# A hybrid S5 / SSD / mLSTM layer: other order of the S5 block's small products, one tile less transposed, S5 steps one slot later

## What is computed

```python
p = h @ W_in                                   # u, z, xbc, dt, qk, v, i, f, o
xbc = silu(causal_conv(xbc, conv_w, conv_b))   # 768 channels x, 256 of B, 256 of C
cb     = einsum('bclgn,bcsgn->bclsg', cm, bm)          # C enters channel-major
states = einsum('bcsgn,bcsgj,bcsgjp->bcgjpn', bm, decay_end, xdt)   # B and x token-major
y_off  = einsum('bclgn,bcgjpn,bclgj->bclgjp', cm, h_prev, exp(acs)) # C channel-major
bu_re  = einsum('blgh,gph->lbgp', ug, bb_re)   # S5: inputs to the states, then a scan
y      = einsum('lbgp,ghp->blgh', s_re, c_re) - einsum('lbgp,ghp->blgh', s_im, c_im)
```

## Time and profile before

| | |
|---|---|
| runs | 2896.5, 2898.15, 2898.3 us; median 2898.15 |
| the profiled execution | 2895.86 us, its span 2894.0 us |
| busy, share of the span | PE 98%, PEld 80%, DVE 66%, ACT 41%, POOL 13% |
| mean granted clock of TensorE | 0.994 of full |
| transfers | 545 MB, mean 188 GB/s |

### The profile page before, as it was taken

How to read it: one execution, slowest core, us unless ns; L and a number is a source line. 1 busy time by engine, 2 the same in 40 slices (tenths; PEclk the granted TensorE clock), 3 DMA queues, 4 the chain that set the end, 5 groups by cost and what they waited for, 6 DMA issues and landing times.

```text
span 2894.0 us, 36039 instructions
## 1 busy us (share of the span) xinstructions
PE 2846.0 (98%) x13576; PEld 2304.7 (80%) x13576; DVE 1903.5 (66%) x2616; ACT 1191.6 (41%) x2005; POOL 386.0 (13%) x496
## 2 busy tenths in 40 slices
PE   8999999999999989999999999999999999999998
PEld 5888888777777767888888788888888888888887
DVE  7677887666853358887343776666866655656656
ACT  6222222454443445545333533333533333545543
POOL 0000000012530236664121100000000000000000
PEclk9999999999999999999999999999999999999999
DMA  4222443446665958887878654444542223866862
GB/s 162 73 73 86 135 132 112 145 143 203 222 198 159 299 173 279 278 300 272 303 268 332 239 197 164 168 153 165 172 172 94 106 98 138 333 194 210 285 195 103
DMA packets 294569, 545.14 MB, mean 188 GB/s; under 512 B 59228, under 2 KB 150780, under 8 KB 284924
## 3 DMA queue, kind: packets, MB, share of 16 engines
q1 hardware_dynamic: 262636, 437.69, 45.2%
q0 software_dynamic: 24704, 75.52, 6.9%
q10 hardware_dynamic: 7056, 29.63, 2.6%
HBM read 358.30 MB, written 184.44 MB: 188 GB/s over the span
## 4 chain that ended last, share of the span: by engine, by line
PE 47%; DVE 2%; DMA 1%; ACT 1%; issue 1%; SPq 0%; DVEq 0%; ACTq 0%
PE f_banks L2985 25%; PE f_banks L2993 14%; PE f_banks L2087 7%; DMA f_h_raw<-hq 1%; PE f_banks L2290 0%; DMA f_bop2lo<-hq 0%; DVE f_snap L2788 0%; DVE f_w_op L2762 0%; DVE f_a L2800 0%; ACT f_w_op L2624 0%; DVE f_a L2795 0%; ACT o_late L2191 0%; ACT f_snap L2642 0%; DVE f_raw L2776 0%; DVE f_bop2lo L2755 0%
## 5 line engine op out<-in xcount | busy, mean ns | idle before, releaser
L2993 PE MATMUL f_banks<-f_d_op 128*128 128x512 f32 x1848 | 419.0, 389 | 0.0
L2993 PEld LDWEIGHTS f_banks<-f_d_op 128*128 128x128 f32 x1848 | 347.1, 188 | 71.8
L2832 DVE TENSOR_TENSOR f_d_op<-f_d_raw,f_d_op 128x1024 fp32r<-128x1024 f32 x154 | 187.4, 1225 | 149.0 <-ACT f_d_op L2663 148.4
L674 PE MATMUL t_banks<-h_hi,c_w_hi 128*128 128x512 f32 x640 | 254.5, 398 | 0.0
L1900 PE MATMUL t_banks<-t_w_hi,h_hi 128*128 128x512 f32 (+1 forms) x640 | 247.9, 387 | 5.1 <-DVE t_w_lo L1761 4.3
L674 PE MATMUL t_banks<-h_hi,c_w_lo 128*128 128x512 f32 x640 | 250.0, 391 | 0.0
L674 PE MATMUL t_banks<-h_lo,c_w_hi 128*128 128x512 f32 x640 | 249.3, 389 | 0.0
L2663 ACT ACTIVATE f_d_op<-f_d_raw 128x1024 fp32r<-128x1024 f32 x154 | 162.8, 1061 | 198.3 <-PE f_banks L2993 161.5
L1900 PE MATMUL t_banks<-t_w_lo,h_hi 128*128 128x512 f32 (+1 forms) x640 | 237.7, 371 | 0.0
L1900 PE MATMUL t_banks<-t_w_hi,h_lo 128*128 128x512 f32 (+1 forms) x640 | 236.8, 370 | 0.0
L2642 ACT ACTIVATE f_snap<-f_banks 128x1024 f32<-128x1024 f32 x88 | 90.3, 1026 | 253.6 <-PE f_banks L2985 253.6
(11 more groups left out here) (410 smaller groups left out, 6293.3 us busy)
## 6 DMA issues: line engine op xcount, KB each, us to landing
f_raw<-in_w_gu SPq DMA_DIRECT2D x88, 512.0 KB, 6.3
sop<-f_a SPq DMA_DIRECT2D x154, 256.0 KB, 2.0
f_d_raw<-sop SPq DMA_DIRECT2D x154, 256.0 KB, 2.9
t_raw<-in_w_tok SPq DMA_DIRECT2D x72, 512.0 KB, 4.6
f_d_raw<-top SPq DMA_DIRECT2D x88, 256.0 KB, 4.4
m_bc<-rows SPq DMA_DIRECT2D x16, 1152.0 KB, 6.8
f_d_raw<-in_w_dn SPq DMA_DIRECT2D x66, 256.0 KB, 3.1
o_y_lo<-y_lo SPq DMA_DIRECT2D x16, 1024.0 KB, 7.8
```

Source lines behind the costliest of these rows:

```text
L674: last = nc.tensor.matmul(banks[:, p % RING, :], w[:, n % 2, k, :], h[:, q, k, :], start=k == 0 and j == 0, stop=k == KD - 1 and j == 2)
L2832: tt(d_op[d % D_RING][:, 2:4], d_raw[:, d % S_RING], d_op[d % D_RING][:, 0:2].bitcast(F32), sub).then_inc(dlo_ok, 1)
L2993: last = nc.tensor.matmul(banks[:, bank, :], d_op[d % D_RING][:, s, tok], d_op[d % D_RING][:, w, :], start=k == 0 and j == 0, stop=k == FU ...
```

## The change

It has three parts. First, two loops of small products are nested the other way, so that consecutive matmuls alternate between the lane groups. The first is in the setup of the lag kernels, the second in `states_in`. Second, tile 8 of the conv tiles (`NOT_TOK = 8`, C of SSD group 0) is no longer transposed, copied and stored; the tiles after it move up one place, `tok_dram` has 11 tiles (`CTT = 11`) and the load of it 1408 columns where it had 1536. Third, `S5_SLOT` is 53.

```diff
-UT, CT, CTT = 4, 16, 12
+UT, CT, CTT = 4, 16, 11
+NOT_TOK = 8
+    def token_piece(c):
+        m, q = divmod(c, BLK)
+        return None if m == NOT_TOK or m > CTT else c if m < NOT_TOK else c - BLK
...
         def transposes(c):
-            if c // BLK < CTT:
+            i = token_piece(c)
+            if i is not None:
                 pe.wait_ge(silu_ok, c + 1)
-                if c >= 2:
-                    pe.wait_ge(tok_ok, c - 1)
+                if i >= 2:
+                    pe.wait_ge(tok_ok, i - 1)
                 for a in range(4):
-                    last = nc.tensor.transpose(tr_banks[:, c % 2, a * P:(a + 1) * P],
+                    last = nc.tensor.transpose(tr_banks[:, i % 2, a * P:(a + 1) * P],
...
-                for g in range(2):
-                    lanes = slice(g * S5P, (g + 1) * S5P)
-                    for q in range(2):
-                        for r, b_in in enumerate((bbr, bbi)):
+                for q in range(2):
+                    for r, b_in in enumerate((bbr, bbi)):
+                        for g in range(2):
+                            lanes = slice(g * S5P, (g + 1) * S5P)
                             last = nc.tensor.matmul(k_banks[g][:, q, :],
...
-X_C, B_C, K_C = 0, XW, XW + NG * NS + NS
+X_C, B_C, K_C = 0, XW, XW + NG * NS
...
-            sp.dma_start(tk[c % 2][:], tok_dram[c * P:(c + 1) * P, :]).then_inc(in_[c % 2], 16)
+            sp.dma_start(tk[c % 2][:, 0:CTT * P], tok_dram[c * P:(c + 1) * P, :]).then_inc(in_[c % 2], 16)
...
-    S5_SLOT, S5_STEP = 52, 2
+    S5_SLOT, S5_STEP = 53, 2
...
-                for e in range(2):
-                    lanes = slice(e * S5P, (e + 1) * S5P)
-                    for r in range(2):
+                for r in range(2):
+                    for e in range(2):
+                        lanes = slice(e * S5P, (e + 1) * S5P)
                         last = nc.tensor.matmul(in_bank[lanes, b, r, :], ...
```

More of the change, by code:

```diff
@@ L254, in send_tok @@
         def send_tok(c):
-            m, q = divmod(c, BLK)
-            if m < CTT:
-                sp.wait_ge(tok_ok, c + 1)
+            i = token_piece(c)
+            if i is not None:
+                m, q = divmod(i, BLK)
+                sp.wait_ge(tok_ok, i + 1)
                 sp.dma_start(tok_dram[q * NB:(q + 1) * NB, m * P:(m + 1) * P].rearrange("(a p) m -> p a m", p=P),
-                             tok[:, c % 2].rearrange("p (a m) -> p a m", m=P)).then_inc(tok_sent[c % 2], 16)
+                             tok[:, i % 2].rearrange("p (a m) -> p a m", m=P)).then_inc(tok_sent[i % 2], 16)
         for q in range(BLK):
@@ L434, in taps @@
             if c >= RING:
-                if m - 1 < CTT:
-                    dve.wait_ge(tr_ok, c - RING + 1)
+                before = token_piece(c - RING)
+                if before is not None:
+                    dve.wait_ge(tr_ok, before + 1)
                 if m - 1 >= CH0:
@@ L448, in token_major @@
         def token_major(c):
-            if c // BLK < CTT:
-                dve.wait_ge(tr_ok, c + 1)
-                if c >= 2:
-                    dve.wait_ge(tok_sent[c % 2], 16 * (c // 2))
-                nc.vector.tensor_copy(tok[:, c % 2], tr_banks[:, c % 2, :]).then_inc(tok_ok, 1)
+            i = token_piece(c)
+            if i is not None:
+                dve.wait_ge(tr_ok, i + 1)
+                if i >= 2:
+                    dve.wait_ge(tok_sent[i % 2], 16 * (i // 2))
+                nc.vector.tensor_copy(tok[:, i % 2], tr_banks[:, i % 2, :]).then_inc(tok_ok, 1)
         tt, ts, stt = nc.vector.tensor_tensor, nc.vector.tensor_scalar, nc.vector.scalar_tensor_tensor
@@ L817, in mixer_memory @@
         part = sb("part", [P, 2, NB])
-        tk1, zo1, va1 = sb("tk1", [P, CTT * P]), sb("zo1", [P, XW + VW]), sb("va1", [P, HM, DA])
+        tk1, zo1, va1 = sb("tk1", [P, (CTT + 1) * P]), sb("zo1", [P, XW + VW]), sb("va1", [P, HM, DA])
         inter, num = sb("inter", [P, 2, HP, DA]), sb("num", [P, 2, HP, DA])
```

2 lines of the change are left out of this document (1 added, 1 removed).

## The result

| | before | changed |
|---|---|---|
| runs, median | 2897.32 us (2896.28 to 2898.3, 4 runs) | 2911.73 us (2910.72 to 2915.81, 4 runs) |
| profiled execution, its span | 2895.86, 2894.0 us | 2910.72, 2908.8 us |
| mean granted clock of TensorE | 0.994 | 0.992 |

The account below looks back on a forecast made before the run. The prediction took TensorE, busy 98% of the span, as the bound. Its terms -1.7 - 3.5 - 1.1 + 2.5 + 2.4 + 0.8 made -0.6 us; 2895.9 - 0.6 + 2.3 = 2897.5 us, range 2891.5 to 2904.

Parts of the forecast that it names:

- (c): SP's S5 loads: u late behind two weight halves in seven steps, 0.35 us each, +2.5 us (0 to +7).
- (d): GLU, fixed at slot 90: TensorE waits longer for g, +2.4 us (ends +1.0 and +2.8).
- (e): TensorE's clock falls to half speed after the longer wait for g, +0.8 us (ends 0 and +1.7).
- Transposes: Tile 8's four pieces lose their transposes on TensorE, 0.43 us each: 1.7 us less.
- lag kernels: Lag kernel setup: alternating lane groups pair at once, 0.44 us a set, eight sets: 3.5 us less (0 to 4.2).
- `states_in` alternating: Inputs to the states: the pairs are there already, so 0, at most 0.2 us either way over 16 steps.
- (a): First S5 step: one slot later, u has long landed and TensorE's wait goes, 1.1 us less.
- (b): VectorE splits both weight halves before every other S5 step, yet states start on time: 0, end +0.5 us.
- The S5 loads become the bound of every other step: Rival for the S5 steps: each of seven u loads 1.0 us too late, +4.9 us, 2903.0 us; chance 0.17.
- The shift is hidden: Rival: u loads still land in time, g's wait grows 1.6 us without a clock dip, 2893.4 us; chance 0.23.
- the order does nothing: Rival: the lag kernels' order changes nothing, as TensorE pairs by its own rule, +2.9, 2901.0 us; chance 0.05.

Follow-up runs that it names:

- experiment 7: The kernel before with only the loop order of the lag kernels changed, so the two lane groups alternate: 2892.2 us, ratio 0.9987.
- experiment 6: The changed kernel with the second weight half of units 15 to 23 loading 64 KB and not 512 KB: 2893.28 us, ratio 0.9990 to before.
- experiment 2: The kernel before with S5_SLOT at 53 and nothing else changed: 2914.79 us, ratio 1.0066.
- experiment 5: The changed kernel with S5_SLOT at 51: 2910.32 us in one run.
- experiment 1: The changed kernel with S5_SLOT back at 52: 2890.66 us, ratio 0.9980 to before.
- 9: The changed kernel with S5_SLOT back at 52 and only the first GLU product moved from slot 90 to 91: 2890.35 us, ratio 0.9968 to before.

## Why the prediction was wrong

The failed step is (c), u's lateness: +2.5 us forecast for the seven steps, and the S5 steps lost 15.7, of which 10.9 are waits for u and 4.7 the half clock at them. Step (d) was too low by 1.9 us, and (e), where all half clock belongs, by 6.9.

*Transposes, lag kernels.* -1.7 and -3.5 forecast, -1.76 and -3.57 measured, and experiment 7 shows that the second reaches the end. That TensorE already ran half of the pairs side by side was read rightly from the windows. `states_in` alternating changed no distance: a step without a wait had 3.14 us of small products in both kernels.

*(a)* The first step waits no more, as forecast, but not because u has "long landed": it was issued at 678.12, landed 6.6 us later, and the product started at 684.90, 0.2 us behind it. The 1.06 us are in the row "to the first S5 step" of the table, with the slot's +2.77 and a shorter wait at 633 us (2.75 for 3.43), which had no stretch at half clock behind it. I had foreseen neither of the last two; they are some 2.4 us of luck.

*(b)* 0 forecast, and it held: VectorE starts the states 0.05 us behind TensorE.

*(c)* I had the right mechanism and the right seven loads, and priced them at +2.5 (end +7) where the S5 steps lost 15.7. I expected u 1.4 to 2.4 us later with 1.4 to spare; in the typical step it came 1.1 us later by its issue and 2.4 by its flight (median 8.6 for 6.2 us of the same q before), 3.5 us. Two things were wrong in it. I wrote that issue and bytes "don't simply add, since the queue has work in the meantime": they do add, as experiment 6 parts them. The queue had hardly a gap to hide either in: from the first weights' issue at 702.25 to u's landing the transfer engines are busy for 0.90 of the time, at 283 GB/s. And I took 512 KB at the saturated rate of 378 GB/s, or from two halves on an empty queue. The row that would have given the price was there: in the earlier trace rows, from SP's weights at 708.88 to u's landing a median of 6.0 us after 710.27, 512 + 528 + 128 + 256 = 1424 KB pass in 7.4 us beside POOL's stores, 193 KB a us. At that pace 512 KB take 2.7 us. With 1.1 us of issue that is 3.8 us, less 1.4 to spare: 2.4 us a step, 17 for seven. Measured were 10.9 and 12.0 in the waits, so this is as much too high as my upper end of 7 was too low; but it says that nearly every one of the seven is late, where I took 0.35 us each. It is too high since u took only 6.7 and 7.0 us for q = 9 and 15, and since it had 7.8 and 7.7 us and not 6.3 for q = 5 and 15. Both of these follow on a stretch at half clock, in which TensorE, and so its need of u, came later. The same is seen in the small waits of 0.5 us in experiment 2 (q = 13) and of 0.4 and 0.2 in experiment 5 (q = 8 and 14), though there the wait for q = 6 is 2.8 us behind such a stretch. The Trainium skill (DMA: Bandwidth & Descriptors, "Queues, rings and completion order") says that each transfer engine takes one queue's descriptors in order and changes between queues packet by packet. The trace agrees: SP's loads kept their order (weights at 707.7 and 710.2 us, record 710.7, kernel 711.5, u 713.7) and shared the engines with POOL's stores.

*(d)* +2.4 forecast (to 3.05 us), 4.94 measured, +4.3. The loads of g took 7.8 us before and 7.9 after, but the last S5 store landed 1.5 us later after its block's start, behind the same traffic. The wait varies between kernels with the same steps, too: 0.65 in before and 1.6 in experiment 1 with the steps at 52, and 3.7 in experiment 2 for 4.94 with them at 53.

*(e)* +0.8 forecast for one dip behind g; there were three, of 3.4, 6.8 and 6.8 us. Without the parts inside waits they cost 4.7 + 3.0 = 7.7 us. I had counted clock only for g, since I expected tenths at each u.

*The rivals.* "The S5 loads become the bound of every other step" is what happened, 0.17 was too little, and its own 1.0 us a step too low as well: over the seven it was 1.6 in waits alone. "The shift is hidden" and "the order does nothing" are refuted. The range was too narrow because its upper end for (c) was a number of the same wrong kind, a rate on a queue that nothing else shares.

## What to carry to other kernels

Before a transfer is put in front of another on a queue, take the queue's own pace from the trace at that very place (bytes from the first issue to the last landing), not the peak rate, and add the later issue to it; compare the sum with the reserve of each transfer behind it. A side task that is moved by a slot keeps its work but changes what stands around it on every list: look at the period of the neighbours (here weights at t = 0 and 1) and at fixed places later (here the GLU). Of two transfers issued together, the one that is needed first goes first; that cost one condition and returned 18.7 us (2911.73 to 2893.04), more than the whole loss of 14.4.

## What the runs showed of the hardware

- Long waits cost twice. At each of the eleven waits of 2.7 to 6.3 us in the S5 steps and the GLU of these runs the granted clock fell to 1.2 GHz for 3.4 or 6.8 us, which costs up to 1.7 or 3.4 us more. Length alone doesn't decide it. Of eight waits of 2.0 to 2.5 us there four were followed by 3.4 us at 1.2 GHz (two in experiment 2, one each in 5 and 9) and four by none (one each in experiment 1 and the changed kernel, two in 2). At the wait for weights near 633 us a length of 2.75 left the clock at 2.4 GHz in the changed kernel, one of 2.73 was followed by 3.4 us in experiment 1, and one of 1.78 too in experiment 7. Why is open.
- 64x16 products of two lane groups overlap where they stand next to each other, also when the program has each group in a row: sixteen in 1.50 us, and in 1.05 us when they alternate.
- The transfer engines were busy for 0.92 of the time at 278 GB/s and for 1.01 at 378: a busy share near one doesn't mean the same rate. Which of the transfers were slower, and why, was not tried.
